# A block chain on one core: both parts of an operand in one matmul in the MLP's first product, another start, and every third low part of the weights made by GpSimd in the stages with heads

## The reference

```python
def first_block(x, meta_tokens, ...):
    h = jnp.concatenate([meta, x], axis=1)                  # 16 + 256 tokens
    h = h + mla_mixer(rmsnorm(h, a_norm_g[j]), ...)         # proj = h @ w_in; 8 heads; y @ w_out
    h = h + rglru_mixer(rmsnorm(h, b_norm_g[j]), ...)       # proj, conv, gates, scan, y @ w_out
    return rmsnorm(h, final_norm_g)[:, N_META:]

def _sq_relu_mlp(h, w_up, w_down):                          # 1024 -> 4096 -> 1024
    u = jax.nn.relu(h @ w_up)
    return (u * u) @ w_down

def second_block(x, mem, ...):
    for layer in range(2):
        z = _rmsnorm(x, norm) @ w_in                        # q, k, v of the heads, q of the memory heads
        o_self = _diff_attention(...) if layer == 0 else _moba_attention(...)
        o_mem = _memory_attention(qm, mem, ...)             # 4 heads of 64 over 256 memory tokens
        x = x + jnp.concatenate([o_self, o_mem], axis=-1) @ w_out[layer]
        x = x + _sq_relu_mlp(_rmsnorm(x, norm_mlp[layer]), w_up[layer], w_down[layer])
    return _rmsnorm(x, final_norm)
```

## Time and profile before

| | us |
|---|---|
| median of 3 runs | 819.76 (819.57 to 819.78) |
| profiled execution | 819.86 |
| its span in the trace | 818.1 |
| PE busy | 804.5 (98%) |
| DVE busy | 582.0 (71%) |
| ACT busy | 531.8 (65%) |
| POOL busy | 0.2 |
| SP's and ACT's transfers, share of 16 DMA engines | 50.4% |

### The profile page before, as it was taken

The page is one execution under the profiler, slowest core; times in us unless marked ns, Lnnn a source line. Parts: engine busy times, 40 slices in busy tenths (PEclk is TensorE's granted clock), DMA queues, the critical chain, the costliest instruction groups (busy, mean ns, idle before and its releaser), DMA issues.

```text
span 818.1 us, 15677 instructions
## 1 busy us (share of the span) xinstructions
PE 804.5 (98%) x6360; PEld 772.2 (94%) x6360; DVE 582.0 (71%) x1073; ACT 531.8 (65%) x977; POOL 0.2 (0%) x4
## 2 busy tenths in 40 slices
PE   8999999999999999999999999999999999999997
PEld 7899999999999899999999999998899998989986
DVE  6999998889988886766545554877758557554734
ACT  6686776599967798655444445679766654545532
POOL 0000000000000000000000000000000000000000
PEclk9999999999999999999999999999999999999999
DMA  9524336565564345375655544453335657555631
GB/s 322 185 87 155 104 107 213 172 206 178 184 207 136 124 154 178 106 258 171 205 191 181 181 150 159 155 180 129 130 104 181 205 182 260 184 197 182 186 100 51
DMA packets 39960, 137.90 MB, mean 169 GB/s; under 512 B 4560, under 2 KB 5328, under 8 KB 39888
## 3 DMA queue, kind: packets, MB, share of 16 engines
q1 hardware_dynamic: 38880, 135.58, 50.4%
q10 hardware_dynamic: 1008, 1.32, 0.5%
HBM read 135.83 MB, written 1.05 MB: 167 GB/s over the span
## 4 chain that ended last, share of the span: by engine, by line
PE 84%; DVE 11%; ACT 2%; issue 1%; DMA 1%; ACTq 0%; DVEq 0%
PE bank L777 21%; PE bank L779 21%; PE bank L778 21%; PE bank L782 5%; PE bank L784 5%; PE bank L783 5%; DVE weights_lo L1686 3%; PE bank L1114 2%; DVE temp L1686 1%; DVE temp L1689 1%; DMA weights_raw<-stream_dram 1%; DVE operand_lo L1686 1%; DVE operand_lo L1692 1%; DVE temp L1892 1%; ACT weights_hi L1192 1%
## 5 line engine op out<-in xcount | busy, mean ns | idle before, releaser
L777 PE MATMUL bank<-operand_hi,weights_hi 128*128 128x256 f32 (+1 forms) x1604 | 458.4, 286 | 2.2 <-DVE weights_lo L1686 1.4
L779 PE MATMUL bank<-operand_hi,weights_lo 128*128 128x256 f32 (+1 forms) x1604 | 454.2, 283 | 0.0
L778 PE MATMUL bank<-operand_lo,weights_hi 128*128 128x256 f32 (+1 forms) x1604 | 454.0, 283 | 0.0
L1192 ACT ACTIVATE weights_hi<-weights_raw 128x1024 fp32r<-128x1024 f32 (+3 forms) x255 | 260.3, 1040 | 158.8 <-PE bank L779 97.9
L1686 DVE TENSOR_TENSOR weights_lo<-weights_raw,weights_hi 128x1024 fp32r<-128x1024 f32 (+3 forms) x255 | 300.1, 1201 | 84.5 <-ACT weights_hi L1192 84.0
L777 PEld LDWEIGHTS bank<-operand_hi,weights_hi 128*128 128x128 f32 x1604 | 303.4, 189 | 8.1 <-issue 4.5
L779 PEld LDWEIGHTS bank<-operand_hi,weights_lo 128*128 128x128 f32 x1604 | 303.8, 189 | 0.0
L778 PEld LDWEIGHTS bank<-operand_lo,weights_hi 128*128 128x128 f32 x1604 | 302.5, 189 | 0.0
L782 PE MATMUL bank<-weights_hi,operand_hi 128*128 128x512 f32 (+1 forms) x300 | 97.5, 325 | 0.0
L784 PE MATMUL bank<-weights_hi,operand_lo 128*128 128x512 f32 (+1 forms) x300 | 96.7, 322 | 0.0
L783 PE MATMUL bank<-weights_lo,operand_hi 128*128 128x512 f32 (+1 forms) x300 | 96.4, 321 | 0.0
(11 more groups left out here) (208 smaller groups left out, 673.9 us busy)
## 6 DMA issues: line engine op xcount, KB each, us to landing
weights_raw<-stream_dram SPq DMA_DIRECT2D x244, 512.0 KB, 4.3
weights_raw<-stream_dram SPq DMA_DIRECT2D x6, 384.0 KB, 4.3
temp<-memT_dram SPq DMA_DIRECT2D x8, 256.0 KB, 4.5
residual<-xT_dram SPq DMA_DIRECT2D x3, 272.0 KB, 5.2
constants<-consts_dram SPq DMA_DIRECT2D x1, 536.5 KB, 8.9
weights_raw<-stream_dram ACTq DMA_DIRECT2D x2, 256.0 KB, 6.1
arena<-consts_dram SPq DMA_DIRECT2D x1, 512.0 KB, 6.2
out_dram<-arena SPq DMA_DIRECT2D x2, 256.0 KB, 2.5
```

The source lines that it names most:

```text
L777: e.matmul(to, w_h, x_h, start=start, stop=False, skip_group_check=True)
L778: e.matmul(to, w_h, x_l, start=False, stop=False, skip_group_check=True)
L779: return e.matmul(to, w_l, x_h, start=False, stop=stop, skip_group_check=True)
L1192: return e.activation(to, of, ACT.Copy, bias=0.0, **scale)
```

## The change

**Start.** The first outputs are four (0 to 3) instead of two, and their units hold two input tiles each: four units, in nine pieces, through banks 0 to 3. All four sums are complete after unit 3. SP and the ACT queue issue the pieces and the input tiles in turn, in order of use. In the first loop of ACT and DVE one piece is split for each input tile, and squares 0 to 3 are made in it; unit 4 is split ahead of squares 4 to 7.

**`up`.** The high and low part of an operand lie in one tensor. The product of a weight tile is two matmuls: the high weights times both parts (512 columns, to both halves of a bank) and the low weights times the high part (256 columns, to the first half). A bank holds one output tile, and the tiles go through banks 5, 6 and 4. When a tile is complete ACT copies the second half to a buffer (`second_sums`, 128 x 256), DVE adds the first half (`add_up`), and relu works on the pair in SBUF.

**Heads.** The scores of the last differential head (score matrices 10 and 11) and its turn come one unit later. The second half of each `out2` product of layer 0 goes input by input instead of output by output.

**GpSimd.** It makes the low part of each third unit (numbers divisible by three) among the last `a_in` units, `a_uq`, `a_k`, `a_v`, `in2`, `v2` and `out2`: units 12, 15, 18 and 21 (12 and 18 have 768 columns), 69 to 93 and 162 to 186, 22 in all. DVE no longer does.

**Table.** The times of all steps of ACT and DVE in `TIMES` are new; one row of it stands in the diff.

The diff, cut to its core:

```diff
-FIRST_WEIGHTS = [(0, 0, 256), (0, 256, 256), (0, 512, 512), (1, 0, 512), (1, 512, 512)]
+FIRST_WEIGHTS = [(0, 0, 256), (0, 256, 256), (0, 512, 512), (1, 0, 512), (1, 512, 512), (2, 0, 512), (2, 512, 512),
+                 (3, 0, 512), (3, 512, 512)]
+FIRST_UNITS = 4
...
-    halves("a_in", 0, 0)
-    rows_of("a_in", 0, range(2, 11))
+    units.extend(Unit("a_in", 0, k0, 2, 0, 4) for k0 in range(0, 8, 2))
+    rows_of("a_in", 0, range(4, 11))
...
-SLOTS_0 = ((7, 9, 11), (8, 10, 12), (13, 15, 18), (14, 16, 19), (17, 19, 20), (17, 19, 21))
+SLOTS_0 = ((7, 9, 11), (8, 10, 12), (13, 15, 18), (14, 16, 19), (17, 19, 20), (18, 20, 21))
...
+def by_gpsimd(v):
+    w = UNITS[v]
+    return v % 3 == 0 and (w.kind in ("a_uq", "a_k", "a_v", "in2", "v2", "out2") or w.kind == "a_in" and w.m0 > 10)
...
-    ("scalar", "root"): (7.5, 13.12, 12.75, 33.2, 38.33, 72.5, 99.5, 165.5, 192.5),
...
+    ("scalar", "root"): (6.5, 11.33, 11.67, 32.25, 36.5, 75.33, 101.5, 166.33, 193.5),
...
-            table["vector"].append((v, len(table["vector"]), ("split_weights", v)))
+            if by_gpsimd(v):
+                table["gpsimd"].append((v, len(table["gpsimd"]), ("split_weights", v)))
+            else:
+                table["vector"].append((v, len(table["vector"]), ("split_weights", v)))
...
-    hold(a + 5.06, range(a + 1, a + 5))
+    hold(a + 5.06, range(a + 3, a + 5))
...
-        op_hi = [sb(f"operand_hi{i}", [P, DT, T1], F32R) for i in range(3)]
-        op_lo = [sb(f"operand_lo{i}", [P, DT, T1], F32R) for i in range(3)]
+        operands = [sb(f"operand{i}", [P, 2, DT, T1], F32R) for i in range(3)]
+        op_hi, op_lo = ([o[:, part] for o in operands] for part in range(2))
...
-                return [(5, 6, 4)[(w.m0 // 2) % 3]]
-            if w.kind == "a_in" and w.m0 < 2:
-                return [0, 1]
+                return [(5, 6, 4)[m % 3] for m in range(w.m0, w.m0 + w.nm)]
+            if w.kind == "a_in" and w.m0 == 0:
+                return [0, 1, 2, 3]
...
+        def up_sum(m):
+            return temp[2 + m // 2 % 3][:, m % 2 * SEQ:(m % 2 + 1) * SEQ]
...
+            def two_sums(b, w_h, w_l, x, start, stop):
+                e.matmul(pair(bank[b][:, 0:2 * SEQ]), w_h, x, start=start, stop=False, skip_group_check=True)
+                return e.matmul(bank[b][:, 0:SEQ], w_l, x[:, 0], start=False, stop=stop, skip_group_check=True)
...
-                for k in range(4):
-                    pe.wait_ge("weights_piece", first_weights_of(v, k))
+                for k in range(2):
                     wait_input(v, w.k0 + k)
                     for j, b in enumerate(bank_of(v)):
+                        pe.wait_ge("weights_piece", first_weights_of(v, k, j))
                         w_h, w_l = weights(v, k, j)
                         i = three(bank[b][:, 0:T1], w_h, w_l, x_h[:, w.k0 + k, :], x_l[:, w.k0 + k, :],
...
-                for j in range(2):
-                    for k in range(4):
-                        tile = OUT2_INPUTS[w.k0 + k] if w.kind == "out2" and w.layer == 0 else w.k0 + k
-                        wait_input(v, tile)
-                        w_h, w_l = weights(v, k, j)
-                        i = three(bank[b][:, j * SEQ:(j + 1) * SEQ], w_h, w_l, x_h[:, tile, 0:SEQ],
-                                  x_l[:, tile, 0:SEQ], j == 0 and w.k0 + k == 0, w.k0 + k == 7)
+                turns = [(j, k) for j in range(2) for k in range(4)]
+                if w.kind == "out2" and w.layer == 0 and w.k0:
+                    turns.sort(key=lambda jk: jk[1])
+                for j, k in turns:
+                    tile = OUT2_INPUTS[w.k0 + k] if w.kind == "out2" and w.layer == 0 else w.k0 + k
+                    wait_input(v, tile)
+                    w_h, w_l = weights(v, k, j)
+                    i = three(bank[b][:, j * SEQ:(j + 1) * SEQ], w_h, w_l, x_h[:, tile, 0:SEQ],
+                              x_l[:, tile, 0:SEQ], j == 0 and w.k0 + k == 0, w.k0 + k == 7)
...
+            def up_tiles(v):
+                w = UNITS[v]
+                x = operands[OPERAND["up", w.layer]]
+                pe.wait_ge("weights_lo", v)
+                for j, b in enumerate(bank_of(v)):
+                    if w.k0 == 0:
+                        take(b)
+                    for k in range(w.nk):
+                        wait_input(v, w.k0 + k)
+                        w_h, w_l = weights(v, k, j)
+                        i = two_sums(b, w_h, w_l, x[:, :, w.k0 + k, 0:SEQ], w.k0 + k == 0, w.k0 + k == 7)
+                    if w.k0 + w.nk == 8:
+                        held_by[b] = [("evacuated", "up", w.layer, w.m0 + j)]
...
+            def second_sums(v):
+                w = UNITS[v]
+                for m, b in zip(range(w.m0, w.m0 + w.nm), bank_of(v)):
+                    if m > 5:
+                        act.wait_ge("hidden", w.layer, m - 6)
+                    else:
+                        act.wait_ge("total", f"mlp_{w.layer}")
+                    act.wait_ge("sum", "up", w.layer, m)
+                    copy(up_sum(m), bank[b][:, SEQ:2 * SEQ], scale=1.0).then_inc(
...
+            act.wait_ge("cleared")
+            split_weights(*FIRST_WEIGHTS[0], piece=0)
             for k in range(DT):
                 input_a(k)
-                for i in [(0,), (1,), (2,), (), (3,), (), (4,), ()][k]:
-                    v, a, size = FIRST_WEIGHTS[i]
-                    split_weights(v, a, size, piece=i)
-            act.wait_ge("cleared")
-            split_weights(2)
-            for k in range(DT):
+                split_weights(*FIRST_WEIGHTS[k + 1], piece=k + 1)
+                if k > 3:
+                    squares_a(k - 4)
+            split_weights(FIRST_UNITS)
+            for k in range(4, DT):
                 squares_a(k)
-                if k in (3, 6):
-                    split_weights(2 + k // 3)
             act.wait_ge("vectors")
             does = {"split_weights": split_weights, "evacuate": evacuate, "root": root, "row": row, "small": small,
...
+            def add_up(v):
+                w = UNITS[v]
+                for m, b in zip(range(w.m0, w.m0 + w.nm), bank_of(v)):
+                    dve.wait_ge("second_sum", w.layer, m)
+                    t = up_sum(m)
+                    tt(t, t, bank[b][:, 0:SEQ], ALU.add).then_inc(*done("added_up", ("evacuated", "up", w.layer, m)))
...
-                if m > 5:
-                    dve.wait_ge("hidden", w.layer, m - 6)
-                dve.wait_ge("sum", "up", w.layer, m + 1)
-                stt(pair(temp[2 + m // 2 % 3][:, 0:512]), pair(bank[bank_of(v)[0]][:, 0:512]), 0.0,
-                    R2.unsqueeze(1).to_broadcast([P, 2, SEQ]), ALU.max, ALU.mult).then_inc(
-                    *done("hidden", ("relu", w.layer, m), ("evacuated", "up", w.layer, m + 1)))
+                for k in (m, m + 1):
+                    dve.wait_ge("evacuated", "up", w.layer, k)
+                t = pair(temp[2 + m // 2 % 3][:, 0:512])
+                stt(t, t, 0.0, R2.unsqueeze(1).to_broadcast([P, 2, SEQ]), ALU.max, ALU.mult).then_inc(
...
+        def gpsimd(e):
+            pool = Lane(e, tally)
+
+            def split_weights(v):
+                size = unit_size(v)
+                pool.wait_ge("weights_hi", v)
+                e.tensor_tensor(w_lo[v % N_SPLIT][:, 0:size], raw[v % N_RAW][:, 0:size],
+                                w_hi[v % N_SPLIT][:, 0:size].bitcast(F32), ALU.subtract).then_inc(
+                    *done("weights_lo_gpsimd", ("weights_lo", v)))
...
-            for i in range(len(FIRST_TILES)):
-                load_tiles(i)
-            load_piece(4)
-            load_weights(2)
+            load_piece(0)
+            load_tiles(0)
+            load_tiles(1)
+            load_piece(3)
+            load_tiles(2)
+            load_piece(5)
+            load_tiles(3)
+            load_piece(7)
+            load_tiles(4)
```

231 lines of the change are left out of this document (128 added, 103 removed), and 44 rows, old and new, of the table TIMES.

## The result

The changed kernel takes 836.67 us (median of 4 runs, 834.1 to 837.52), the kernel before in the same comparison 819.77 (819.57 to 820.08): a ratio of 1.020, 95% interval 1.0188 to 1.0213. It is **16.9 us slower**; 813.4 was forecast, with 5% for slower. The profiled run took 837.52 us.

What follows compares the result with a forecast made beforehand. PE's work and waits were taken to bound the kernel, VectorE running neck and neck with PE to 121.47 us. Gains 2.2 + 2.0 + 1.9 + 0.3 = 6.4 us from 819.86, less 0.1, gave 813.4 us; range 809.0 to 818.4.

Steps and rivals of the forecast that it cites:

- What bounds the kernel: Whole kernel: PE busy for 804.5 of 818.1 us, so time comes only from PE's work and PE's waits.
- A, `up`: MLPs: a long and a short matmul per product make each unit 0.034 us shorter, -2.2 us over 64 units.
- B, the start: Start to 121.47 us: -1.0 us for the first norm's mean, -0.6 from idle time the new table of times fills.
- B, GpSimd: First layer's heads: four low parts leave VectorE, 4.34 us, less 3.9 for VectorE held half of 1.96 each: -0.4 us.
- The table of times: Start to 121.47 us: new times can fill VectorE's 3.5 us of idle time, of which 0.6 was taken.
- C: Layer 0 of the second block: later score matrices 10 and 11 give 1.2 us, `out2` order 0.7: -1.9 us.
- D: Rest, head stages of the second block: small waits partly go beside 18 GpSimd operations, -0.3 us, bounds -1.2 and +2.
- The same, and slower than before: Rival, 5%: GpSimd takes 2.70 us and holds VectorE throughout; +5.5 first layer and start, +2 later heads, 823 us.
- Its turning point: VectorE's queue, units 11 to 23: sign turns at about 2.1 us held per GpSimd operation.
- The argument against VectorE being held: Against the rival with VectorE held, 12%, 819.2 us: VectorE works on banks half of that time, may not want what GpSimd uses.

Runs made afterwards that it cites:

- experiment 5: Changed kernel with VectorE making all low parts and the old times for ScalarE and VectorE between units 11 and 99 and 160 and 192: 818.16 us, ratio 0.9980.
- Experiment 2: Kernel before with only GpSimd's low parts of the same 22 units added, old table of times kept: 830.67 us, ratio 1.0133.
- experiment 1: Changed kernel with VectorE making all low parts again and GpSimd idle, new table of times kept: 834.78 us, ratio 1.0189.
- experiment 3: Changed kernel with GpSimd's 22 operations treating only 16 columns each, the rest of those low parts left out: 813.41 us, ratio 0.9926.

## Why the prediction was wrong, point by point

**What bounds the kernel**: right. PE's work and waits, VectorE behind the waits; each large wait of the changed kernel is for VectorE.

**A, `up`: right, a little small.** A unit takes 2.793 us from its first matmul to that of the next, so the pair of a long and a short matmul 0.349 (433.38 to 433.73 below; 0.351 was forecast). The two MLPs gain 1.44 and 1.32 us between units 96 and 160 and from 186 to the end, 2.8 for the forecast 2.2. No wait for a bank or for `add_up` appeared.

```profile
433.38 0.40 PE L812 MATMUL bank<-operand,weights_hi 128*128 128x512 f32 x1
433.61 0.28 PE L813 MATMUL bank<-operand,weights_lo 128*128 128x256 f32 x1
433.73 0.39 PE L812 MATMUL bank<-operand,weights_hi 128*128 128x512 f32 x1
```

**B, the start: right in sum, wrong by term.** Unit 6 starts 1.6 us sooner, for 1.0 + 0.6. But the mean moved by 0.4 us only (20.39 for 20.76), and 1.2 came from the wait at the spread, so the sum is right in part by luck. What I did not see is that this gain lasts only as long as VectorE is relieved behind it (experiment 5).

**B, GpSimd: the step that failed.** Three things in it. *Its duration*: 1,024 columns take 2.4 us when nothing delays them and 768 take 1.85; 1.96 was the midpoint, the upper bound 2.70 was near. The estimate of 2.25 from the Trainium skill's figure ("GPSIMD Engine Reference", 3.1 Elementwise — side-by-side cycle accounting) was nearer than the midpoint. *The share for which VectorE is held*: VectorE's busy time rose by 607.5 - 577.7 = 29.8 us, 1.35 per operation, 0.56 of its length; half of the midpoint was assumed, 0.98. *The account itself*: I priced the holding as work on VectorE's queue, against the work taken off it, and let it take up free time in the later stages. By that account the measured holding would be a loss of 29.8 - 26.3 = 3.5 us in all. Experiment 2 refutes it: VectorE is busy for as long as before, and 10.9 us are lost. A low part that VectorE makes stands at a planned place in its queue and takes 1.22 us; GpSimd's begins when the high part is there, which no table sets, and then a step of a head stands still for up to 2.2 us, with PE behind it. So the sum had no term for when.

**The table of times: a step that was missing.** I argued that the new times can only fill idle time (0.6 us). They are built on a VectorE that no longer makes the 22 low parts and leave no room for anything else: 21.4 us between experiments 1 and 3, for 1.4 in the old table. That relief is worth at most PE's waits of before held in the old order (1.4 us, of 5 us of waits), but the new order's loss when the relief fails has no such bound.

**C: right.** Score matrices 10 and 11 take 0.93 us with no wait, for 1.47 and 0.83:

```profile
318.61 0.93 PE L1180 MATMUL bank<-arena 64*128 64x128 f32 x8
```

From unit 84 to 87 experiment 3 gains 1.0 us, from 90 to 93 another 0.7 by the order of `out2`, as worked out; together 1.7 for 1.9. In the changed kernel the first is 0.5, since VectorE is late.

**D: wrong by sign.** Forecast -0.3 with a bound of +2; the heads of layer 1 lost 10.2 us and those of layer 0 5.3 with C's gain in it. The 50 us that VectorE has free there were no cover: in the places seen a head's step is held and PE waits behind it, whatever VectorE has free before and after.

**The rivals.** "The same, and slower than before" named the holding and had 5%. For the first layer its +5.5 us is near the 7.0 measured (3.4 of which come without GpSimd, in experiment 1); for the later stages its +2 is over 13 us short, for the same reason as D, and nothing in it stands for the table. Its turning point, 2.1 us held per operation, was far too high: 1.35 gave +17 us. The argument against VectorE being held was a misreading: it was said to work on banks half of the time. In the trace of before, from 57.33 to 121.47 us, instructions that name a bank are 22 of the 73 us of VectorE's instructions (their lengths summed), and two-input instructions without a bank are 33.

The time without GpSimd's work, 813.4 in experiment 3, is the number that was forecast. That it agrees to the last digit is luck in part. By the table, units 6 to 24 lose 0.5 us there, where a gain was forecast, and the MLPs and layer 1's heads gain more than they were given. But the sum shows that the forecast was about the time of a kernel in which the helper is free.

What stays open: the old table loses 10.9 us by GpSimd with VectorE's busy time unchanged. That it is the moment at which it is held, and not the sum, fits the places seen and the MLPs (22.9 us held, 1.5 us lost), but is not shown. No run set these moments, which would take an order in which GpSimd waits for a step of VectorE.
